# Experts that go twice over their weights: down products of both blocks in turns by halves of the contraction, and the first such expert as fourth letter

## What is computed

```
logits = (xf @ w_router).astype(jnp.float32) + b_router.astype(jnp.float32)
top_val, top_idx = lax.top_k(logits, TOP_K)
gates = jax.nn.softmax(top_val, axis=-1)
...
hu = xb @ w_up[e] + b_up[e]
x_glu = jnp.minimum(hu[:, :D_FF], SWIGLU_LIMIT)
x_lin = jnp.clip(hu[:, D_FF:], -SWIGLU_LIMIT, SWIGLU_LIMIT)
act = x_glu * jax.nn.sigmoid(SWIGLU_ALPHA * x_glu) * (x_lin + 1.0)
return act @ w_down[e] + b_down[e]
```

## Time and profile before

| | us |
|---|---|
| median of 3 runs | 2625.54 (2620.56 to 2626.98) |
| span of the profiled execution | 2629.4 |
| TensorE busy in it | 2418.1 (92%) |
| VectorE busy | 958.8 (36%) |
| ScalarE busy | 558.8 (21%) |
| GpSimd busy | 212.7 (8%) |
| memory read and written | 535.72 MB and 26.35 MB |

### The profile page before, as it was taken

One profiled execution on the slowest core, in us unless ns is written; L12 is line 12 of the kernel. 1 busy time (PEld: TensorE's weight loads), 2 busy tenths in 40 slices (PEclk: granted clock), 3 DMA queues, 4 the chain that ended last, 5 costly groups with the idle time before them and its releaser, 6 DMA issues. The chain is left out here.

```text
span 2629.4 us, 27726 instructions
## 1 busy us (share of the span) xinstructions
PE 2418.1 (92%) x10465; PEld 1162.8 (44%) x10465; DVE 958.8 (36%) x2103; ACT 558.8 (21%) x1291; POOL 212.7 (8%) x381
## 2 busy tenths in 40 slices
PE   5988999959999989799999997999998789999999
PEld 2534587443343333333333333656444344454443
DVE  2666364371212112111211112615465764341462
ACT  1254432010000000000000001212355452210350
POOL 1000253001010100010010001100000000000000
PEclk8988999969999999999999998999889999999999
DMA  9200396619999999998999899220000002112000
GB/s 342 82 32 32 134 346 250 249 52 386 427 424 427 427 426 427 423 402 330 412 412 413 346 426 364 95 92 33 0 1 1 0 1 88 48 64 96 1 33 32
DMA packets 122993, 563.99 MB, mean 214 GB/s; under 512 B 18997, under 2 KB 42990, under 8 KB 95074
## 3 DMA queue, kind: packets, MB, share of 16 engines
q1 hardware_dynamic: 104600, 517.55, 49.0%
q0 software_dynamic: 15360, 39.43, 4.0%
q10 hardware_dynamic: 2890, 5.13, 0.6%
HBM read 535.72 MB, written 26.35 MB: 214 GB/s over the span
## 5 line engine op out<-in xcount | busy, mean ns | idle before, releaser
L1845 PE MATMUL ps<-ring,mem 128*32 128x512 f32 (+2 forms) x1680 | 391.6, 618 | 24.6 <-issue 24.6
L218 PE MATMUL ps<-mem,ring 128*128 128x512 f32 (+1 forms) x992 | 396.2, 559 | 2.6 <-DVE mem L796 1.6
L218 PE MATMUL ps<-ring,mem 128*128 128x512 f32 (+5 forms) x1136 | 382.8, 493 | 8.8 <-ACT mem L2945 3.7
L218 PEld LDWEIGHTS ps<-mem,ring 128*128 128x128 f32 x992 | 189.7, 193 | 197.8 <-issue 189.1
L218 PEld LDWEIGHTS ps<-ring,mem 128*128 128x128 f32 x1136 | 196.9, 192 | 178.1 <-issue 153.7
L224 PE MATMUL ps<-mem 128*128 128x128 f32 (+2 forms) x1155 | 194.4, 302 | 58.8 <-DVE mem L2762 10.7
L1845 PEld LDWEIGHTS ps<-ring,mem 128*32 128x32 f32 (+2 forms) x1680 | 134.6, 137 | 242.6 <-issue 240.7
L224 PEld LDWEIGHTS ps<-mem 128*128 128x128 f32 (+2 forms) x1155 | 148.9, 167 | 184.8 <-issue 114.7
L1845 PE MATMUL ps<-mem 128*32 128x512 f32 (+2 forms) x752 | 197.9, 604 | 3.5 <-issue 3.5
L1910 PE MATMUL ps<-mem 128*32 128x512 f32 (+2 forms) x672 | 178.1, 597 | 2.2 <-DVE mem L1954 1.8
L1910 PE MATMUL ps<-ring,mem 128*32 128x512 f32 (+2 forms) x736 | 171.0, 601 | 8.8 <-issue 8.8
(11 more groups left out here) (389 smaller groups left out, 2482.3 us busy)
## 6 DMA issues: line engine op xcount, KB each, us to landing
ring<-in_w_up SPq DMA_DIRECT2D x75, 2048.0 KB, 19.6
mem<-in_w_up SPq DMA_DIRECT2D x37, 2048.0 KB, 20.4
ring<-in_w_down SPq DMA_DIRECT2D x33, 2048.0 KB, 25.6
mem<-in_w_down SPq DMA_DIRECT2D x31, 2048.0 KB, 24.3
ring<-in_w_up SPq DMA_DIRECT2D x56, 512.0 KB, 15.4
ring<-in_w_ada SPq DMA_DIRECT2D x12, 2048.0 KB, 9.2
ring<-in_mod_w SPq DMA_DIRECT2D x8, 2048.0 KB, 14.9
ring<-in_cd_w_in SPq DMA_DIRECT2D x6, 2048.0 KB, 7.8
```

The source lines that it names most:

```text
L218: i = e.matmul(o, l, r, start=(start and n == 0), stop=(stop and n == len(pairs) - 1))
L1845: m = e.matmul(PS[n][c0:c0 + rows, :], XGT[:, u, k * 128 + c0:k * 128 + c0 + rows], wt[:, kk, n * 512:n * 512 + 512], start=False, stop=(k ...
```

## The change

PLAN is `SPQESSPQSPQPSQPEQSP` instead of `SPQSSPQSPQPESQPEQSP`: the first E moves from the twelfth place to the fourth. The blocks from number 13 on are the same as before.

In an E, the two down products are now made in turns (`pe_down_both`): first half of the contraction for the first block, then for the second block, second half for the first, then for the second. The second block's sums go to banks 2 and 3, the first block's to 6 and 7 as before. The tiles of the first half are given back after the second turn, those of the second half after the fourth. The loads of an E's down tiles come in the order first halves of both experts, then second halves. The transposes that stood beside the down rounds stand after the turns. The up behind an E waits for the copies of y before its bias products for banks 2 and 3. `act_copy_y` takes the first block's y after the third turn and the second block's from banks 2 and 3.

```
-PLAN = "SPQSSPQSPQPESQPEQSP"
+PLAN = "SPQESSPQSPQPSQPEQSP"
...
             yield "up", i
-            if i and not blocks[i - 1].again:
+            if b.again:
+                yield "both", i
+            elif i and not blocks[i - 1].again:
                 yield "down", i - 1
-            if b.again:
-                yield "down", i
...
-    def pe_up(e, L, i, parts, between):
+    def pe_up(e, L, i, parts, between, again=False):
...
         for n in range(4):
+            if n == 2 and again:
+                e.wait_ge(L.y_copied, 2 * i)
...
+    def pe_down_both(e, L, a, parts, between):
+        e.wait_ge(L.y_copied, 2 * a)
+        for q in range(2):
+            for b in range(2):
+                at, bank0 = (Y[:, (a + 1) % 2, :], 2) if b else (ACTT, 6)
+                wts = []
+                for b_, c0, rows, x, tile in parts:
+                    if b_ == b:
+                        wt, ready = tile(4 + q)
+                        e.wait_ge(*ready)
+                        wts.append((c0, rows, x, wt.rearrange("p (k n) -> p k n", n=1024)))
+                e.wait_ge(L.a_copied, 2 * (a + q) + b + 1)
+                if q == 0:
+                    for n in range(2):
+                        for c0, rows, x, wt in wts:
+                            bias_product(e, PS[bank0 + n], x, n, 1, c0, rows)
+                for kk in range(4):
+                    k = 4 * q + kk
+                    for n in range(2):
+                        for c0, rows, x, wt in wts:
+                            m = e.matmul(PS[bank0 + n][c0:c0 + rows, :], at[:, k * 128 + c0:k * 128 + c0 + rows],
+                                         wt[:, kk, n * 512:n * 512 + 512], start=False, stop=(k == 7))
+                m.then_inc(L.down, 1)
+                between(q, b)
...
-    def act_copy_y(e, L, i):
-        e.wait_ge(L.down, 2 * (i + 1))
+    def act_copy_y(e, L, i, half=None):
+        e.wait_ge(L.down, 2 * (i + 1) + (1 if half == 0 else 0))
...
-            e.activation(Y[:, i % 2, n * 512:n * 512 + 512], PS[6 + n], ACT.Copy).then_inc(L.y_copied, 1)
+            e.activation(Y[:, i % 2, n * 512:n * 512 + 512], PS[(2 if half == 1 else 6) + n], ACT.Copy).then_inc(L.y_copied, 1)
...
+            def beside_both(q, b):
+                if q == 0:
+                    pe_turn_a(e, main, i, b)
+                    if b == 1:
+                        pe_turn_x(e, main, i + 1, 0)
+                elif b == 0:
                     pe_turn_x(e, main, i + 1, 1)
...
+            elif what == "both":
+                pe_down_both(e, main, i - 1, both_parts(i), beside_both)
+                for q in range(2):
+                    give_back(ps, 4 + q, (main.down, 2 * (i - 1) + 2 * q + 2))
```

More of the change, by code:

```diff
@@ L1882, in pe_turn_a, with pe_down @@
                        for q in range(4)]).then_inc(L.a_turned, 1)
[L1884 to L1893, removed]
+    def pe_down(e, L, i, parts, between=lambda q: None):
         if i:
@@ L1904, in pe_down @@
                 wts += [(c, r, wt.rearrange("p (k n) -> p k n", n=1024)) for c, r in tiles(c0, rows)]
-            e.wait_ge(L.a_copied, copied[q])
+            e.wait_ge(L.a_copied, 2 * i + q + 1)
             for kk in range(4):
@@ L1909, in pe_down @@
                     for c0, rows, wt in wts:
-                        m = e.matmul(PS[6 + n][c0:c0 + rows, :], at[:, k * 128 + c0:k * 128 + c0 + rows], wt[:, kk, n * 512:n * 512 + 512],
+                        m = e.matmul(PS[6 + n][c0:c0 + rows, :], ACTT[:, k * 128 + c0:k * 128 + c0 + rows], wt[:, kk, n * 512:n * 512 + 512],
                                      start=False, stop=(k == 7))
@@ L2054, in beside_down @@
                     pe_turn_x(e, main, i + 3, q)
[L2055 to L2059, removed]
+            def beside_both(q, b):
[4 more added lines that the diff above has]
+                elif b == 0:
                     pe_turn_x(e, main, i + 1, 1)
             if what == "up" and h is None:
-                pe_up(e, main, i, parts(i), beside_up)
+                pe_up(e, main, i, parts(i), beside_up, i > 0 and blocks[i - 1].again)
                 for q in range(4):
@@ L2073, in pe_experts @@
                     pe_turn_a(e, main, i, 1)
-                pe_down(e, main, i, parts(i), h, beside_down)
+                pe_down(e, main, i, parts(i), beside_down)
                 for q in range(2):
-                    if h != 0:
-                        give_back(ps, 4 + q, (main.down, 2 * i + q + 1))
+                    give_back(ps, 4 + q, (main.down, 2 * i + q + 1))
     def dve_experts(e):
@@ L2113, in act_experts @@
             if i and not blocks[i - 1].again:
-                act_copy_y(e, main, i - 1)
+                act_copy_y(e, main, i - 1, blocks[i - 1].half)
             if i == NMAIN - 2:
@@ L2121, in act_experts @@
             if blocks[i].again or i == NMAIN - 1:
-                act_copy_y(e, main, i)
+                act_copy_y(e, main, i, blocks[i].half)
         e.wait_ge(main.y_copied, 2 * NMAIN)
```

## The result

The changed kernel takes 2633.6 us (median of 12 runs, 2628.8 to 2637.6); the ratio to the kernel before, from runs side by side, is 1.0055 (95% interval 1.0038 to 1.0073), so it is 10 to 19 us slower. In a later comparison the ratio was 1.0042 (1.0024 to 1.0060), 6 to 16 us. The medians of the first comparison lie closer together: the kernel before took 2625.8 us in its 12 runs, or 2623.0 without the two slow ones of 3367 and 9978 us, so by them the change costs 8 or 11 us. The predicted time was 2632.5 us, but the prediction called "within 0.3%" the likeliest outcome, and that was wrong.

A forecast was written before the change was run, and what follows sets the result against it. DMA was taken to set the second E's start: 11 us later, tail 5.1 earlier, switches +0.5, giving +6.4, taken as +7 on the median 2625.5, so 2632.5 us; range 2619 to 2640.

The forecast's parts named there:

- within 0.3%: Whole kernel: too little change to tell, either a little later (+1 to +8 us) or 2620.5 us; chance 0.54 together.
- What bounds the kernel: At the second E, first matmul waits 1.08 us for a weight tile, so transfers, not TensorE, set the time there.
- Ring full behind the early E: Two S behind the early E: eight slots cap the lead at seven tiles, DMA idles 28 us, second E 11 later.
- The waits that return: Between 1050 us and the second E: TensorE's waits for weights come back later, 40 to 48 us in all.
- The wait at the early E's start: At about 720 us TensorE has no stock and waits some 2 us for E's first pair of tiles.
- The turns' own prices: In each E: tiles released after 15.4 us, not 24.5; 0.88 and 0.23 gaps gone; copy wait 1.1; switches 0.25.
- The tail: Behind the second E: one tile 4.9 us earlier removes 5.1 us of wait and slow matmuls; TensorE late next.
- B: Slower: ring full through E S S, tail saves little; +8 to +13 us, about 2636; chance 0.38.
- the bound at 7.9: Whole kernel: 0.3%, 7.9 us, is about what a measurement can tell from no change.
- C: DMA idles no more than before and the tail gives 5 us back: 2620.5 us; chance 0.11.
- D: Faster: the early E's stock lasts into P and Q, ending 36.4 us of waits; 2578 at most; chance 0.08.

The follow-up runs named there:

- the order P, S, Q without the turns: Kernel before with PLAN SPQEPSQSPSQPSQPEQSP and the old down products; ratio to the kernel before 1.0001 (0.9985 to 1.0016).
- the order P, S, Q behind the E: Changed kernel, turns kept, with PLAN SPQEPSQSPSQPSQPEQSP: P, S, Q instead of two S behind the early E; ratio to the kernel before 0.9958.
- the orders with a P or Q behind each early E: PLANs SPQEPSQSPSQPSQPEQSP and SPQEPSQPEQSPSQSPQSP, ratios to the kernel before: 0.9958 and 0.9927 with the turns, 1.0001 and 0.9994 on the kernel before without them.

## Why the prediction was right or wrong

**What bounds the kernel: right.** The second E's start is a wait for DMA in every trace here, and it moved as the idle time of the DMA before it.

**Ring full behind the early E: right in place and in size.** 28 us of idle DMA were predicted, from 830 to 925. The trace lost 26.7 us from 826 to 926, and the P behind the two S starts at 909.5 (912 predicted). The second E was to come 11 us later (7 to 13). From the stage's start it is 10.3 and 11.5 us later in the two pairs of traces. The waits that return were given as 40 to 48 us and are 46.8. The wait at the early E's start is 0.69 us and not 2.

**The turns' own prices: right.** Release at 16.0 us (15.4 predicted), the wait for copies 0.87 us (1.1), the gaps of 0.88 and 0.23 us gone. The 0.25 us per E for two more changes between 128 and 64 columns did not show: the downs of an E became shorter by 1.4 us, of which the two gaps are 1.1.

**The tail: this is the step that failed.** The prediction took 5.1 us off behind the second E: 3.48 of wait and 1.6 of slower matmuls at the last up tile, which one more tile in time, 4.9 us, should take away, so that TensorE itself would be late next. From the second E to the end, the stage takes 255.1 and 251.9 us in the two traces of the kernel before and 251.8 and 250.8 in the changed kernel's. So 3.3 and 1.1 us were won between these pairs. Turns alone gave 3.1 us by the ratio, and turns in the new order 14.4 - 11.0 = 3.4. Three things were wrong in that term.

First, the tile does not come 4.9 us earlier. Counted from the second E, the last up tile started at 215.9 and 214.3 us in the kernel before and at 212.8 and 211.4 in the changed one, about 3 us earlier. Part of the tile is thrown away in the last S, where a pause of 5.6 us opened (4.7 with the turns alone): the same full ring that the prediction had described for the first E. From the pause at the second E to that point the changed kernel loses 6.0 + 5.6 = 11.6 us, the kernel before 11.9.

Second, TensorE was not late next. The wait at the last up tile fell to 0.68 us and its tile to 7.09, but a wait for the last down tile came, 1.21 us; all five traces with the turns, eight slots and these last letters show it (0.93 to 1.21), and none of the four without the turns.

Third, the price came from one execution. The row is no accident, since the order alone shows 3.43 and 8.70 again, but the second trace of the kernel before has only 2.36 us to win there, and the order P, S, Q without the turns 1.98.

**The sum and the chances.** 11 - 3 is +8, and not +6.4 taken as +7. The ratios say 11 and 14. Eight lies inside the interval of one comparison (6 to 16) and under that of the other (10 to 19), so up to 6 us are not explained by the steps. The stages of the traces differ by 7.0 and 10.4 us, which is the shift of the second E less what the tail won. The case that came is nearest to B, slower by 8 to 13 with little saved in the tail, to which I gave 0.38, after 0.54 for "within 0.3%"; its condition, 11 us later with under 3 saved, is met by the second pair of traces and just missed by the first. With a point forecast at +7 and the bound at 7.9, most of the weight of the tail's doubt lay above the bound, since 5.1 was the most the tail could save. I had it the wrong way round. That 2632.5 lies so near to 2633.6 is partly luck: the ratio of 1.0055 belongs to a kernel before of about 2619, not 2625.5, and the change itself, +14 by that ratio, was forecast at half its size.

**C and D.** Neither an unchanged idle time nor a lasting stock was seen. But D's thought, that waits for weights in P and Q go, comes true with a P behind the E. From the fourth letter to the second E these waits are 37.5 us in the kernel before, 47.5 in the changed one, and 27.1 in the order P, S, Q behind the E.

**What stays open.** The 3 to 6 us between the steps and the middle of the ratios. The layers behind the experts do not hold them in the traces: 1005.5 and 1002.5 us in the kernel before, 1003.1 and 991.6 in the changed one. In the other experiments too the ratio and the stage of the one trace differ by up to 6 us, in both directions. How often an execution of the kernel before has the longer wait in the last P is not known from two traces.

## What to carry to other kernels

In a pipeline with a ring of N slots, sum up transfer time and compute time piece by piece in the order of the program. Stock is what the transfers have loaded ahead of the compute; pieces in which the compute is slower (compute-bound) buy it only up to N - 1 tiles, and what they would buy beyond that is lost and paid back later as waits. So alternate pieces that use stock with pieces that build it, and look at an early release of slots only together with what follows it; it was worth 3 us where compute-bound pieces followed, and in the orders with a P or Q behind each early E 6 and 12 us by the stages, 11 and 18 by the ratios. Do not take a saving from a single short wait of one trace: take its size from a second trace, or keep zero as its likely value.

## What the runs showed that I had not expected

Outside the changed stage, the same program differed by 11 us between two executions. Here are the layers behind the experts in both traces of the changed kernel, columns as before:

```profile
1630.30:2633.40 1003.10, 937.27 (x3233) 490.04 (x3232) 480.81 (x1184) 327.34 (x736) 23.17 (x29) 0.95 0.12 44
```

```profile
1631.30:2622.90 991.60, 926.57 (x3232) 486.97 (x3232) 480.41 (x1184) 327.13 (x736) 23.99 (x29) 0.96 0.13 44
```

The number of matmul records is the same to one, the granted clock is 0.95 in one and 0.96 in the other, and TensorE is busy for 937 and 927 us. Both stages of experts take 1038 us. A difference of 10 us between two spans says nothing about this change; the stage by itself does.
